# Eight low parts of the first mixer's weights made by VectorE, where GpSimd made them

## The chip, the cores and the metric

The kernel runs on one core of a Trainium2 chip. The metric is the device time of one execution in microseconds. Times of single instructions come from one profiled execution.

## The reference

Two transformer blocks over 256 tokens of width 1024 in float32. The change lies in the first mixer of the first block, which computes

```python
h = rmsnorm(x, norm1_w)
rq, rk, rv, rg, mq, mk, mv, ga, gb = split(h @ w_in)      # widths 512 512 1024 1024 512 512 512 1024 1024
ret = silu(rg) * retention(rotary(rq), rotary(rk), rv)    # 4 heads, chunks of 128
a = ret @ w_ret_out
b = moba_attention(rmsnorm(mq), rmsnorm(mk), mv) @ w_moba_out   # 8 heads of 64; with 256 tokens one block, causal softmax
x = x + (sigmoid(ga) * a + sigmoid(gb) * b) @ w_o
```

Behind it come a gated feed-forward of width 2816, and the second block: four more such feed-forwards, a forgetting attention, a latent attention (MLA) and two gated side inputs. All products are wanted at float32 precision.

## The kernel before

**Split products.** TensorE multiplies rounded float32 (fp32r). Each float32 weight is therefore split in two: a high part, its rounding, and a low part, the weight less the high part; activations are split likewise. A product is the sum of three matmuls (`mm3`, lines 582 to 584): high by high, high by low, low by high.

**Units.** All weights come through a list of 252 units (`weight_units`), in the order of their use, most of 128 x 2048 numbers: one MB, in two DMAs of 512 KB that SP issues. A unit u goes through three raw buffers (`w_raw[u % 3]`) and four buffers of high and low parts (`slots[u]`). ScalarE makes the high part (line 1326 in `split_to`, counted by `w_hi_done`) once the unit has landed and the unit before it in its slot has been used. VectorE (`lo`, line 1859) or GpSimd (line 507) makes the low part and counts up `w_lo_done[u % 3]`. TensorE waits for that count before it uses the low part, and SP waits for it before it loads unit u + 3 into the same raw buffer. `pool_units` is the set of units whose low part GpSimd makes; VectorE skips these in its own `split_to`, GpSimd's loop skips all others.

**Order on each engine.** Every engine runs one list of instructions in the order in which it is written. `split_to(n)` issues the parts of all units below n that aren't issued yet; `ahead(stage)` is `split_to` up to three units past the stage's last one. On VectorE these calls stand between the other work: `ahead("mv0")` ahead of the scaling of the MoBA queries and keys (line 2224 is its first instruction: mean and epsilon for the inverse roots), `split_to(unit_at["ga0"][0] + RING)` between the gating of the retention (line 2271) and the attention, and in the attention one unit per head, through this list:

```python
            fill = {s: [lambda u=u: split_to(u + RING)] for s, u in
                    zip((0, 1, 2, 3, 4, 7, 8), [*unit_at["ga0"], *unit_at["ga1"], *unit_at["gb0"], *unit_at["gb1"]][1:])}
```

The entries of key s run on VectorE after the softmax and the scaling of head s + 1.

**Units around the change** (each stage here has two units, moba_out0 and moba_out1 have one): rq0 0, 1; rk0 2, 3; rv0 4, 5; rv1 6, 7; mq0 8, 9; mk0 10, 11; mv0 12, 13; rg0 14, 15; rg1 16, 17; ga0 18, 19; ga1 20, 21; gb0 22, 23; gb1 24, 25; ret_out0 26, 27; ret_out1 28, 29; moba_out0 30; moba_out1 31; w_o 32 to 35; the feed-forward from 36.

**MoBA attention.** `attention("moba", ...)` runs a pipeline over heads. In step s TensorE makes the scores of head s (line 893, into bank 4 or 5), transposes the weights of head s - 1 (line 578, once VectorE has scaled them), for every second head multiplies a pair of heads by their values (line 915), and then fills in projections: step 0 the second unit of ga0, steps 1 and 2 ga1, 3 the first unit of gb0, 4 and 5 the second of gb0 (a tile of tokens each) with transposes of the retention's output in step 4, 6 only such transposes, 7 and 8 gb1. VectorE, per head: masked scores and their maximum (line 2085), the reciprocal of the sum (line 2092), the scaling of the weights (line 2096), for every second head the low part of an output (line 2104), and what `fill` holds. ScalarE, per head: what its own `fill` holds (the high part of a unit, the tanh of a gate), the exponentials (line 1334, like most of its work), a copy of the turned weights and of an output. The high part of unit 25 stands in its list ahead of the tanh of gb0 and the exponentials of head 6, behind the exponentials of head 5.

Of the kernel before, what the change touches and what calls it, by code (L numbers as in the profile page):

```python
# [48 lines left out]
RMS_EPS, LN_EPS, GN_EPS = 1e-6, 1e-5, 1e-5  # L49
ALPHA = float((2 * 2) ** 0.25)  # L50
NEG = -1e30
POOL_STAGES = ("ga1", "gb0", "gb1", "kv_up", "fox_q1", "fox_k1", "fox_q2", "fox_k2", "fox_v5", "fox_q3", "fox_k3", "uq",
               "mla_oa0", "mla_oa1")

F32 = mybir.dt.float32
# [124 lines left out]
def build(nc, dram, marks):  # L180
# [3 lines left out]
    units, unit_at = weight_units(dram)  # L184
# [14 lines left out]
    def up_cols(f):  # L199
        return slice(HB - gate_cols(f).start, 2 * HB - gate_cols(f).start)  # L200

    pool_units = {u for u, unit in enumerate(units) if unit[0] in POOL_STAGES}
    pool_units |= {unit_at[f"ffn{f}"][0] + 1 for f in (0, 1, 2, 4)}
    pool_units |= {unit_at[stage][i] for stage, i in (("rg0", 1), ("moba_out1", 0), ("fox_v4", 0),
                                                      ("fox_o0", 0), ("fox_o1", 0),
                                                      ("ple_g00", 0), ("ple_g10", 0))}
    ffn_w = [(dram["w_ffn_gate"], dram["w_ffn_up"], dram["w_ffn_down"])]
# [2325 lines left out]
```

## Time and profile before

| | us |
|---|---|
| median of 3 runs | 1500.1 (1499.11 to 1500.71) |
| the profiled execution | 1500.31 |
| its span, first to last instruction | 1498.2 |
| TensorE busy | 1477.7 |
| VectorE busy | 928.7 |
| ScalarE busy | 793.2 |
| GpSimd busy, 56 instructions | 190.1 |

The profile follows one execution. PE is TensorE, DVE VectorE, ACT ScalarE, POOL GpSimd, SP the engine whose queue issues the loads of weights. L2271 is line 2271 of the kernel. A matmul's end is modelled, so neighbouring ones overlap in the rows. Times are microseconds from the start of the span unless marked ns. The mean granted clock of TensorE is 0.998 of full speed.

### The profile page before, as it was taken

How to read it: one execution, taken by the hardware profiler on the slowest of the kernel's cores; microseconds unless marked ns; L12 is line 12 of the kernel's file. 1: busy time of each engine (PE TensorE's matmuls, PEld its weight loads, DVE VectorE, ACT ScalarE, POOL GpSimd, SP SyncE). 2: the span in 40 equal slices, each digit the busy share in tenths (PEclk: the TensorE clock that was granted, in tenths of full speed). 3: DMA queues.
4: the chain of work that ended last, by engine and by line, in shares of the span. 5: the costliest groups of instructions: out<-in, count | busy, mean ns of one | idle time of the engine just before them, and what ended most of it. 6: DMA issues, size and time to landing. Idle time of an engine off the chain costs nothing.

```text
span 1498.2 us, 21332 instructions
## 1 busy us (share of the span) xinstructions
PE 1477.7 (99%) x8040; PEld 1275.1 (85%) x8040; DVE 928.7 (62%) x1207; ACT 793.2 (53%) x975; POOL 190.1 (13%) x56
## 2 busy tenths in 40 slices
PE   8999999999999999999999999999999999999997
PEld 6888788888888888888888888888888998888886
DVE  7476455666656665525766668765666565766667
ACT  6436545444444445666544456644446664544456
POOL 0015211000040000372100001000005441100010
PEclk9999999999999999999999999999999999999999
DMA  9545456666546555552565557565555336555562
GB/s 345 185 142 177 135 177 198 217 195 196 186 159 214 184 186 177 187 170 85 196 222 183 186 194 228 176 223 184 186 192 164 124 113 197 196 197 188 184 216 71
DMA packets 187545, 274.73 MB, mean 183 GB/s; under 512 B 10048, under 2 KB 137184, under 8 KB 187488
## 3 DMA queue, kind: packets, MB, share of 16 engines
q1 hardware_dynamic: 183568, 262.77, 53.3%
q10 hardware_dynamic: 3920, 11.18, 2.3%
q8 instruction: 39, 0.64, 0.2%
q14 instruction: 18, 0.15, 0.0%
HBM read 272.83 MB, written 1.05 MB: 183 GB/s over the span
## 4 chain that ended last, share of the span: by engine, by line
PE 91%; DVE 5%; ACT 2%; issue 1%; DMA 0%; DVEq 0%; SPq 0%; ACTq 0%
PE bank L720 23%; PE bank L727 12%; PE acc L584 7%; PE acc L583 7%; PE acc L582 7%; PE bank L582 6%; PE bank L584 6%; PE bank L583 6%; PE bank L766 3%; PE acc L893 2%; PE acc L578 2%; PE bank L629 2%; PE bank L636 2%; PE bank L644 2%; DVE w_lo L1859 1%; PE bank L951 1%
## 5 line engine op out<-in xcount | busy, mean ns | idle before, releaser
L1859 DVE TENSOR_TENSOR w_lo<-w_raw,w_hi 128x2048 fp32r<-128x2048 f32 (+1 forms) x208 | 472.9, 2278 | 165.6 <-ACT w_hi L1410 121.3
L720 PE MATMUL bank<-xT,w_hi 128*128 128x512 f32 x1520 | 361.3, 390 | 0.0
L507 POOL TENSOR_TENSOR w_lo<-w_raw,w_hi 128x2048 fp32r<-128x2048 f32 (+1 forms) x41 | 176.9, 4321 | 1264.9 <-ACT w_hi L1326 1264.9
L720 PEld LDWEIGHTS bank<-xT,w_hi 128*128 128x128 f32 x1520 | 282.6, 188 | 56.6
L1410 ACT ACTIVATE w_hi<-w_raw 128x2048 fp32r<-128x2048 f32 x145 | 276.4, 1906 | 0.0
L1326 ACT ACTIVATE w_hi<-w_raw 128x2048 fp32r<-128x2048 f32 (+4 forms) x105 | 189.4, 1817 | 29.1 <-PE bank L584 10.1
L727 PEld LDWEIGHTS bank<-xT,w_lo 128*128 128x128 f32 x1520 | 189.3, 192 | 3.9
L727 PE MATMUL bank<-xT,w_lo 128*128 128x256 f32 x1520 | 191.4, 284 | 0.0
L582 PE MATMUL acc<-w_hi,sTh 128*128 128x512 f32 x400 | 155.9, 390 | 0.0
L583 PE MATMUL acc<-w_lo,sTh 128*128 128x512 f32 x400 | 155.9, 390 | 0.0
L584 PE MATMUL acc<-w_hi,sTl 128*128 128x512 f32 x400 | 155.8, 390 | 0.0
L582 PE MATMUL bank<-w_hi,xT 128*128 128x512 f32 (+1 forms) x304 | 119.8, 394 | 0.2 <-DVE w_lo L1859 0.2
L584 PE MATMUL bank<-w_hi,xT 128*128 128x512 f32 (+1 forms) x304 | 117.1, 385 | 0.0
L583 PE MATMUL bank<-w_lo,xT 128*128 128x512 f32 (+1 forms) x304 | 116.9, 384 | 0.0
L1421 ACT ACTIVATE squares<-bank 128x512 f32<-128x512 f32 x50 | 29.9, 597 | 139.6 <-PE bank L727 139.6
L1432 ACT ACTIVATE sTh<-hid 128x512 fp32r<-128x512 f32 x45 | 28.4, 632 | 135.0 <-PE acc L584 135.0
L584 PEld LDWEIGHTS acc<-w_hi,sTl 128*128 128x128 f32 x400 | 75.1, 188 | 15.6
L582 PEld LDWEIGHTS acc<-w_hi,sTh 128*128 128x128 f32 x400 | 75.1, 188 | 15.4
L583 PEld LDWEIGHTS acc<-w_lo,sTh 128*128 128x128 f32 x400 | 75.1, 188 | 15.4
L1421 ACT ACTIVATE tanh<-bank 128x512 f32<-128x512 f32 x45 | 26.8, 596 | 106.2 <-PE bank L720 106.2
L582 PE MATMUL bank<-xT,w_hi 128*128 128x256 f32 x271 | 78.7, 290 | 0.3 <-ACT arena L1334 0.3
L584 PE MATMUL bank<-xT,w_lo 128*128 128x256 f32 x271 | 76.8, 283 | 0.0
(231 smaller groups left out, 2030.0 us busy)
## 6 DMA issues: line engine op xcount, KB each, us to landing
w_raw<-in_ffn_w_in SPq DMA_DIRECT2D x176, 512.0 KB, 4.4
w_raw<-in_ffn_w_out SPq DMA_DIRECT2D x88, 512.0 KB, 4.2
w_raw<-in_w_in SPq DMA_DIRECT2D x52, 512.0 KB, 4.8
w_raw<-in_fox_w_in SPq DMA_DIRECT2D x24, 512.0 KB, 4.6
w_raw<-in_w_ffn_gate SPq DMA_DIRECT2D x22, 512.0 KB, 4.7
w_raw<-in_w_ffn_up SPq DMA_DIRECT2D x22, 512.0 KB, 4.5
w_raw<-in_w_ffn_down SPq DMA_DIRECT2D x22, 512.0 KB, 4.2
w_raw<-in_ple_w_gate SPq DMA_DIRECT2D x16, 512.0 KB, 4.5
```

The lines of the kernel that those rows point to most:

```text
L507: pool.tensor_tensor(w_lo[s][:, 0:cols], w_raw[u % RING][:, 0:cols], w_hi[s][:, 0:cols].bitcast(F32), ALU.subtract).then_inc(w_lo_done[u % ...
L578: mm = pe.matmul(bank[b][:, c:c + P], src, ident, is_transpose=True, start=True, stop=True)
L582: pe.matmul(out, ah, bh, start=first, stop=False, skip_group_check=biased)
L583: pe.matmul(out, ah, bl, start=False, stop=False, skip_group_check=biased)
L584: return pe.matmul(out, al, bh, start=False, stop=last, skip_group_check=biased)
L720: mm = pe.matmul(bank[b + m], wh[:, k, m], both, start=k == 0 and not narrow_first, stop=k == KD - 1 and narrow_first, skip_group_check=na ...
L727: mm = pe.matmul(bank[b + m][:, S:], wl[:, k, m], xTh[:, k], start=k == 0 and narrow_first, stop=k == KD - 1 and not narrow_first, skip_gr ...
L766: mm = pe.matmul(out, (xTl if part == 1 else xTh)[:, k, tok], both[:, k], start=part == 0 and k == 0, stop=last and k == KD - 1)
L1326: nc.scalar.activation(hi, raw, ACT.Copy).then_inc(w_hi_done, 1)
L1410: nc.scalar.activation(w_hi[slots[u]][:, :], w_raw[u % RING][:, :], ACT.Copy).then_inc(w_hi_done, 1)
L1421: nc.scalar.activation(dst.rearrange("p (m n) -> p m n", m=2), low[:, b:b + 2, S:], ACT.Copy)\
L1859: nc.vector.tensor_tensor(w_lo[s][:, 0:cols], w_raw[u % RING][:, 0:cols], w_hi[s][:, 0:cols].bitcast(F32), ALU.subtract).then_inc(w_lo_don ...
```

## The change

The set `pool_units` loses eight units of the first mixer: the second unit of rg0 (15), both of ga1 (20, 21), of gb0 (22, 23) and of gb1 (24, 25), and that of moba_out1 (31). Since VectorE's `split_to` takes every unit that isn't in the set, VectorE issues these eight low parts, each where its `split_to` reaches the unit's number. The instruction is the same on the other engine. GpSimd keeps the units behind the first mixer.

```diff
-POOL_STAGES = ("ga1", "gb0", "gb1", "kv_up", "fox_q1", "fox_k1", "fox_q2", "fox_k2", "fox_v5", "fox_q3", "fox_k3", "uq",
+POOL_STAGES = ("kv_up", "fox_q1", "fox_k1", "fox_q2", "fox_k2", "fox_v5", "fox_q3", "fox_k3", "uq",
                "mla_oa0", "mla_oa1")
...
-    pool_units |= {unit_at[stage][i] for stage, i in (("rg0", 1), ("moba_out1", 0), ("fox_v4", 0),
+    pool_units |= {unit_at[stage][i] for stage, i in (("fox_v4", 0),
                                                       ("fox_o0", 0), ("fox_o1", 0),
                                                       ("ple_g00", 0), ("ple_g10", 0))}
```

## Rows read from the trace of the kernel before

**Rows 1.** The page: busy time of each engine, and the chain that ended last.
```profile
PE 1477.7 (99%) x8040; PEld 1275.1 (85%) x8040; DVE 928.7 (62%) x1207; ACT 793.2 (53%) x975; POOL 190.1 (13%) x56
...
PE 91%; DVE 5%; ACT 2%; issue 1%; DMA 0%; DVEq 0%; SPq 0%; ACTq 0%
```

**Rows 2.** The page's costliest groups: busy us, mean ns; idle before, and its releaser.
```profile
L1859 DVE TENSOR_TENSOR w_lo<-w_raw,w_hi 128x2048 fp32r<-128x2048 f32 (+1 forms) x208 | 472.9, 2278 | 165.6 <-ACT w_hi L1410 121.3
...
L507 POOL TENSOR_TENSOR w_lo<-w_raw,w_hi 128x2048 fp32r<-128x2048 f32 (+1 forms) x41 | 176.9, 4321 | 1264.9 <-ACT w_hi L1326 1264.9
```

**Rows 3.** Waits of TensorE, 60 to 260 us: us in total, times, longest.
```profile
PE acc L578 <- DVE arena L2096: 1.1, 2, 0.8
```

**Rows 4.** Timeline of GpSimd: start, us taken, instruction, count, idle before.
```profile
86.62 4.90 POOL L507 TENSOR_TENSOR w_lo<-w_raw,w_hi 128x2048 fp32r<-128x2048 f32 x1 [83.58 <-ACT w_hi L1326]
122.97 5.03 POOL L507 TENSOR_TENSOR w_lo<-w_raw,w_hi 128x2048 fp32r<-128x2048 f32 x1 [31.45 <-ACT w_hi L1326]
132.67 9.18 POOL L507 TENSOR_TENSOR w_lo<-w_raw,w_hi 128x2048 fp32r<-128x2048 f32 x2 [4.67 <-ACT w_hi L1326]
...
161.28 4.55 POOL L507 TENSOR_TENSOR w_lo<-w_raw,w_hi 128x2048 fp32r<-128x2048 f32 x1 [7.46 <-ACT w_hi L1326]
192.79 5.12 POOL L507 TENSOR_TENSOR w_lo<-w_raw,w_hi 128x2048 fp32r<-128x2048 f32 x1 [26.96 <-ACT w_hi L1326]
```

**Rows 5.** Timeline of VectorE ahead of the attention.
```profile
84.77 2.29 DVE L1859 TENSOR_TENSOR w_lo<-w_raw,w_hi 128x2048 fp32r<-128x2048 f32 x1 [1.59 <-ACT w_hi L1326]
86.97 4.59 DVE L2224 TENSOR_SCALAR rsqrt_v<-rsqrt_b 128x32 f32<-128x32 f32 x1
...
119.93 1.41 DVE L2271 SCALAR_TENSOR_TENSOR arena<-tanh,neg_mean,arena 128x512 f32<-128x512 f32 x2
...
124.78 4.44 DVE L2271 SCALAR_TENSOR_TENSOR arena<-squares,neg_mean,arena 128x512 f32<-128x512 f32 x2
129.14 0.28 DVE L2085 CUSTOM_DVE_ANT_0 arena<-acc,mask 128x128 f32<-128x128 f32 x1
```

**Rows 6.** Timeline of ScalarE: high parts of units 14, 15 and of 25.
```profile
82.83 3.71 ACT L1326 ACTIVATE w_hi<-w_raw 128x2048 fp32r<-128x2048 f32 x2
...
159.30 1.91 ACT L1326 ACTIVATE w_hi<-w_raw 128x2048 fp32r<-128x2048 f32 x1
```

**Rows 7.** Timeline of VectorE in the attention: heads 2, 4, 5 and 6.
```profile
138.56 0.29 DVE L2085 CUSTOM_DVE_ANT_0 arena<-acc,mask 128x128 f32<-128x128 f32 x1 [2.97 <-PE acc L893]
...
154.38 0.74 DVE L2096 TENSOR_SCALAR arena<-acc,exp_rsum 128x128 f32<-128x128 f32 x2
157.09 0.29 DVE L2085 CUSTOM_DVE_ANT_0 arena<-acc,mask 128x128 f32<-128x128 f32 x1 [1.97 <-PE acc L893]
...
161.83 0.29 DVE L2085 CUSTOM_DVE_ANT_0 arena<-acc,mask 128x128 f32<-128x128 f32 x1 [1.77 <-PE acc L893]
...
163.73 0.74 DVE L2096 TENSOR_SCALAR arena<-acc,exp_rsum 128x128 f32<-128x128 f32 x2
```

**Rows 8.** Timeline of TensorE: scores and transposes of weights in three steps.
```profile
130.69 0.82 PE L893 MATMUL acc<-arena 128*128 128x128 f32 x4
131.82 0.55 PE L578 MATMUL acc<-ident,arena 128*128 128x128 f32 x3 [0.32 <-DVE arena L2096]
...
160.98 0.82 PE L893 MATMUL acc<-arena 128*128 128x128 f32 x4
161.63 0.49 PE L578 MATMUL acc<-ident,arena 128*128 128x128 f32 x3
...
162.90 0.82 PE L893 MATMUL acc<-arena 128*128 128x128 f32 x4
164.53 0.55 PE L578 MATMUL acc<-ident,arena 128*128 128x128 f32 x3 [0.80 <-DVE arena L2096]
```

**Rows 9.** Windows at the end: length, busy of each engine, granted clock, DMA.
```profile
1490.00:1492.00 2.00, 0.00 (x0) 0.00 (x0) 1.76 (x8) 1.88 (x4) 0.00 (x0) 1.00 0.00 0
1492.00:1494.00 2.00, 0.00 (x0) 0.00 (x0) 1.38 (x4) 1.46 (x3) 0.00 (x0) 0.86 0.00 0
```

## Prediction

> **What bounds the kernel now.** I read the page first: TensorE is busy for 1477.7 of 1498.2 us, and the chain that ended last is 91% TensorE, 5% VectorE and 2% ScalarE [rows 1]. So work taken from or given to another engine counts only where TensorE waits for it. The groups then give the price of a low part: 2278 ns on VectorE and 4321 ns on GpSimd (4.6 us for a unit of 2048 columns, the mean holds shorter ones) [rows 2]. The waits between 60 and 260 us, the stretch that holds all eight moved units, show what there is to win: TensorE stood for 1.1 us, two times, before transposes of softmax weights (line 578) that VectorE had to scale (line 2096), the longer time 0.8 us [rows 3]. The timeline of GpSimd says when the moved parts run now [rows 4], those of VectorE and ScalarE what stands beside them [rows 5 to 7], and that of TensorE where the two waits lie [rows 8]: the first pair of transposes of the MoBA attention at 131.82 and the seventh at 164.53. I count heads from 0, and units as the list of the kernel does: 15 is the second of rg0, 20 and 21 ga1, 22 and 23 gb0, 24 and 25 gb1, 31 moba_out1.
>
> **What is removed.** GpSimd loses eight instructions: units 15, 20, 21 and 22 (one row of 9.18), 23, 24, 25 and 31. Nothing else is in its queue there: its next instruction, for unit 37 at about 234, is for the feed-forward, and stays. No DMA, no matmul and no ScalarE instruction is added or removed. SP's loads wait for low parts (three raw buffers), so they shift; I come to that.
>
> **What is added.** Eight instructions of line 1859 on VectorE. Back to back one takes the queue for 2.20 us (84.77 to 86.97) [rows 5]. That is 17.6 us of VectorE in a stretch where it is busy for little more than half. Each stands at the place where its loop calls `split_to`, and holds up whatever comes behind it until ScalarE's high part is there.
>
> **Unit 15 and the lock.** It now stands in front of line 2224. Its high part is the second of the two of ScalarE that begin at 82.83 and end at 86.54 [rows 6], so it runs from 86.97 to 89.17. Today line 2224, a scalar operation on 32 columns, takes 4.59 us from 86.97, to 91.56 [rows 5], and the GpSimd unit that began at 86.62 ends at 91.52 [rows 4]: I read this as VectorE held until GpSimd is through. Without it the line should take some 0.2 us, so VectorE is at 89.4 where it now is at 91.56: 2.2 us early although it does more.
> The Trainium skill, "SBUF — State Buffer", section "SBUF: two separate sides", says that GpSimd and VectorE share one pair of ports as an exclusive lock for a whole instruction, against VectorE operations in a two-port mode or with two SBUF inputs. The trace agrees here, with 4.59 us for line 2224.
>
> **Unit 20 and the first softmax.** The same shows at line 2271: the pair at 119.93 takes 1.41 us, the same shape at 124.78 takes 4.44 [rows 5], beside the GpSimd unit that runs from 122.97 to 128.00 [rows 4]. That is 3.03 us given back, for one unit of 2.20. Even if none of the 2.2 us won at unit 15 were left (VectorE waits several times for ScalarE and TensorE in between), VectorE would be through line 2271 at 124.78 + 1.41 = 126.2 and through unit 20 at 128.4, before the 129.14 at which the first softmax begins now; if all of it is left, at 126.2. So the weights of head 0 come 0.8 to 3.0 us earlier. TensorE uses 0.48 of it: in a step without a wait the transposes begin 0.65 us after the scores (160.98 to 161.63), so at 130.69 + 0.65 = 131.34 where it is 131.82 today [rows 8]. Term: -0.48 us. More can't come of it: TensorE has no other wait before this.
>
> **Units 21, 22, 23.** In the attention VectorE makes unit 21 after the weights of head 1, 22 after those of 2, 23 after those of 3. It then stands idle till TensorE has the next scores: 2.97 us before 138.56, and more the two times after it [rows 7]; a unit of 2.20 fits each time. TensorE asks for each one or two steps later, with a margin of over 2 us. Cost 0, covered by this idle time; with the cover gone each would cost up to 2.20.
>
> **Unit 24.** The weights of head 4 end at 154.38 + 0.74 = 155.12, and the softmax of head 5 begins at 157.09, 1.97 later [rows 7]. The unit ends at about 157.26: 0.17 us late. TensorE isn't waiting there, but ScalarE's exponentials of head 5 and its high part of unit 25 behind them are late by as much.
>
> **Unit 25, the one that costs.** Its high part is made by ScalarE from 159.30 to 161.21 [rows 6], behind the exponentials of head 5, the turned weights and the output of a pair; GpSimd starts at 161.28 [rows 4]. The softmax of head 6 begins at 161.83 [rows 7], as soon as TensorE has the scores (from 160.98, four matmuls in 0.82). In the new order unit 25 stands ahead of that softmax and waits for its high part till 161.21 + 0.17 = 161.38; it runs from 161.42 to 163.62, and only then the softmax begins: 163.62 - 161.83 = 1.79 us late. TensorE has no large fill in this step, only transposes and the scores of head 7 (from 162.90), and already waits 0.80 for the weights of head 6 [rows 8]. So the whole 1.79 goes into the path: softmax, exponentials and scaling take 2.64 from 161.83 to 163.73 + 0.74 [rows 7], the transposes begin at 166.3. Term: +1.79 us; without the 0.17 of unit 24 1.62. Bounds: 0, if something lets ScalarE make the high part earlier (nothing in its order does), and 1.79 + 0.5 if the queue of ScalarE, which evacuates the gates between, is held up too.
>
> **Unit 31 and the loads.** GpSimd makes it from 192.79, when its high part is there [rows 4]; on VectorE it follows unit 30, and TensorE uses it only behind the rest of ret_out1 and the whole of moba_out0. Cost 0; without that cover 2.20. The raw buffers come free later for units 22, 23 and 24, in which units 25, 26 and 27 are loaded. Unit 22 is through at about 138.56 + 2.64 + 2.20 = 143.4 (a softmax and its scaling take 2.64, below), some 1.5 us later than now; a load lands about 5 us after its issue; and ScalarE converts unit 25 at 159.30 [rows 6], 11 us behind. Unit 24 is through at 157.3, so unit 27 lands by about 163, and ScalarE takes 26 and 27 only behind the transposes of 164.53 [rows 8]. Cost 0; if one of these loads were over its slack, ScalarE and then TensorE would wait for the excess.
>
> **Sum.** The profiled execution took 1500.31 us, its span is 1498.2, 2.1 lie around it, and it is 0.2 above the median of 1500.1. So 1500.31 - 0.48 + 1.79 = 1501.6, and on the scale of the median 1501.4: 1.3 us, or 0.09%, slower. Behind the attention TensorE, the other engines and the loads are all tied to each other, and I see nothing that would take a delay back.
>
> The Trainium skill, "GPSIMD Engine Reference", section "Engine selection", advises VectorE for elementwise work, GpSimd being about two times slower. The trace agrees, with 4.6 [rows 4] against 2.28 us [rows 2], but the place in VectorE's queue decides: by the page alone the change would be a gain, and I weigh that as the first rival.
>
> **Rivals.** A measurement of this kernel can tell about 0.2%, 3 us, from no change.
> *The gain alone.* The lock's end gives 0.48 us and unit 25 costs nothing, because the softmax of head 6 isn't late or the delay is taken back behind it: 1499.6. For it: VectorE gets over 7 us of held time back. Against: that time lies before 129.14, and the wait at 164.53 exists already [rows 8]. If all 1.1 us of waits for weights [rows 3] went too: 1499.0, so a gain of over 0.2% is out of reach by this road.
> *No lock (the other side).* The 4.59 and 4.44 us are long for another reason and stay. Then units 15 and 20 come on top, 4.4 us, the weights of head 0 are 4.4 us later, and TensorE waits for them: 1500.1 + 4.4 + 1.8 = 1506.3. It decides, as slower by over 0.2%, once the weights of head 0 come 1.2 us later than now. Against it: the ends of both long operations follow those of the GpSimd units, and line 2096, which reads PSUM, takes 0.74 both beside GpSimd (163.73) and without it (154.38) [rows 4, 7].
> *The clock falls.* The pause at 163.7 grows from 0.8 to 2.6 us. At the end of the kernel the granted clock falls from 2.4 to 1.2 GHz only after TensorE has stood since 1490: 1.00 till 1492, 0.86 in the next two [rows 9], so some 3.7 us of idleness were borne at the high level. Should it fall after 2.6, each us at 1.2 GHz costs half a us, and 3.4 us there make it slower by over 0.2%; 8 us would give 1505.4.
>
> **How the numbers follow.** Forecast 0.80, gain alone 0.09, no lock 0.06, clock 0.05. The forecast's own spread (1.62 to 2.3 for unit 25, 0 to 0.48 won, and some 0.8 of scatter of a median, as the three runs show) is 1500.3 to 1503.0. The range reaches down to the first rival: 1499.5 to 1503.0. Slower by over 0.2%, above 1503.1: the last two rivals and the forecast's upper edge, 0.12. Faster by over 0.2%, below 1497.1: no case, 0.03 for what I missed. Within 0.2%: 0.85.
>
> **What would show it.** GpSimd busy about 152 us (190.1 less the eight units: 4.90, 5.03, 9.18 for two, 4.55, 5.12 and two of 4.6 [rows 4]) with 48 instructions; line 1859 216 times; VectorE at 928.7 + 18.2 - 7.4 = 939.5 us (eight of 2.28, less 4.4 and 3.0). Line 2224 at about 0.2 us, the second pair of line 2271 at 1.4. No wait of TensorE at 131, one of about 2.6 us at 163 to 166, and unit 25 on VectorE right before the softmax of head 6. Wrong, if that softmax still begins with its scores; if line 2224 stays long; if new waits of TensorE stand between 132 and 158, or before the ret_out and moba_out matmuls.

## The result, and the profile after

The median of 22 runs is 1502.81 us (1500.36 to 1504.07) against 1500.09 (1499.11 to 1500.96), slower by 2.7 us or 0.18%. The means lie 2.1 us apart, a ratio of 1.0014 with a 95% interval of 1.0008 to 1.0020: clear of noise, and inside the 0.2% that I had called no change. The 22 runs aren't one heap: ten lie from 1500.36 to 1501.18, none between 1501.2 and 1502.7, and twelve from 1502.71 to 1504.07. The profiled execution, 1503.06 us with a span of 1501.2, is one of the upper group.

The page of the changed kernel, busy times and the two costliest groups (columns as in [rows 1, 2]):

```profile
PE 1479.3 (99%) x8040; PEld 1275.8 (85%) x8040; DVE 938.5 (63%) x1215; ACT 793.6 (53%) x975; POOL 152.1 (10%) x48
...
L1859 DVE TENSOR_TENSOR w_lo<-w_raw,w_hi 128x2048 fp32r<-128x2048 f32 (+1 forms) x216 | 490.9, 2278 | 168.9 <-ACT w_hi L1410 121.4
...
L507 POOL TENSOR_TENSOR w_lo<-w_raw,w_hi 128x2048 fp32r<-128x2048 f32 (+1 forms) x33 | 138.9, 4216 | 1305.9 <-ACT w_hi L1326 1305.9
```

GpSimd and VectorE are where the forecast put them (152 and 939.5 us). Waits of TensorE from 60 to 260 us in the changed kernel, answering to [rows 3]:

```profile
PE acc L578 <- DVE arena L2096: 2.4, 1, 2.4
PE acc L915 <- ACT squares L1334: 0.7, 1, 0.7
PE bank L582 <- DVE w_lo L1859: 0.2, 1, 0.2
```

One wait for scaled weights in place of two, and longer than both together. The timeline of VectorE ahead of the attention, answering to [rows 5]:

```profile
85.08 4.50 DVE L1859 TENSOR_TENSOR w_lo<-w_raw,w_hi 128x2048 fp32r<-128x2048 f32 x2 [1.59 <-ACT w_hi L1326]
89.50 0.17 DVE L2224 TENSOR_SCALAR rsqrt_v<-rsqrt_b 128x32 f32<-128x32 f32 x1
...
122.87 1.41 DVE L2271 SCALAR_TENSOR_TENSOR arena<-squares,neg_mean,arena 128x512 f32<-128x512 f32 x2
124.20 2.28 DVE L1859 TENSOR_TENSOR w_lo<-w_raw,w_hi 128x2048 fp32r<-128x2048 f32 x1
126.40 0.28 DVE L2085 CUSTOM_DVE_ANT_0 arena<-acc,mask 128x128 f32<-128x128 f32 x1
```

Units 14 and 15 run back to back, line 2224 takes 0.17 us where it took 4.59, the second pair of line 2271 takes 1.41 where it took 4.44, and with unit 20 in between the first softmax begins at 126.40 instead of 129.14. Then the attention, VectorE at heads 5 and 6 (answering to [rows 7]), with units 24 and 25:

```profile
154.80 2.28 DVE L1859 TENSOR_TENSOR w_lo<-w_raw,w_hi 128x2048 fp32r<-128x2048 f32 x1
156.99 0.28 DVE L2085 CUSTOM_DVE_ANT_0 arena<-acc,mask 128x128 f32<-128x128 f32 x1
...
161.13 2.29 DVE L1859 TENSOR_TENSOR w_lo<-w_raw,w_hi 128x2048 fp32r<-128x2048 f32 x1 [1.17 <-ACT w_hi L1326]
163.34 0.28 DVE L2085 CUSTOM_DVE_ANT_0 arena<-acc,mask 128x128 f32<-128x128 f32 x1
```

VectorE waits 1.17 us for ScalarE's high part of unit 25, spends 2.2 on the low part, and only then, at 163.34, begins the softmax whose scores TensorE began at 160.74. TensorE in the same steps (answering to [rows 8]):

```profile
131.01 0.82 PE L893 MATMUL acc<-arena 128*128 128x128 f32 x4
131.66 0.49 PE L578 MATMUL acc<-ident,arena 128*128 128x128 f32 x3
...
160.74 0.82 PE L893 MATMUL acc<-arena 128*128 128x128 f32 x4
161.39 0.49 PE L578 MATMUL acc<-ident,arena 128*128 128x128 f32 x3
...
162.79 0.82 PE L893 MATMUL acc<-arena 128*128 128x128 f32 x4
166.03 0.74 PE L578 MATMUL acc<-ident,arena 128*128 128x128 f32 x3 [2.41 <-DVE arena L2096]
...
179.87 0.38 PE L578 MATMUL acc<-ident,arena 128*128 128x128 f32 x2
```

And the row of the kernel before that answers to the last one, the transposes of head 7:

```profile
176.82 0.49 PE L578 MATMUL acc<-ident,arena 128*128 128x128 f32 x3
```

Subtracting row from row of [rows 8] gives the account. The scores of head 1 are 131.01 - 130.69 = 0.32 us late: the execution was that much behind before the attention. Those of head 6 are 160.74 - 160.98 = 0.24 early: 0.56 won at head 0. The transposes of head 6 are 166.03 - 164.53 = 1.50 late: 1.74 lost at unit 25. The transposes of head 7 are 179.87 - 176.82 = 3.05 late: another 1.55, in a stretch where TensorE waited for nothing. The windows say why (columns as in [rows 9]):

```profile
164.00:166.00 2.00, 0.00 (x0) 0.00 (x0) 0.94 (x4) 1.99 (x7) 0.00 (x0) 1.00 0.73 226
166.00:168.00 2.00, 1.98 (x11) 1.11 (x11) 1.71 (x6) 0.59 (x2) 0.00 (x0) 0.56 0.79 298
168.00:170.00 2.00, 2.00 (x9) 1.50 (x6) 1.20 (x5) 2.00 (x7) 0.00 (x0) 0.59 0.00 0
170.00:172.00 2.00, 2.00 (x11) 1.63 (x10) 2.00 (x4) 1.19 (x1) 0.00 (x0) 1.00 0.00 0
```

The granted clock fell to its lower level, 1.2 GHz, about when the pause ended, and came back to 2.4 before 170. A mean between 1.00 and 0.50 is a mixture of the two levels: 0.56 and 0.59 over two stretches of 2 us are 3.4 us at the lower one. At half speed these would cost 1.7 us of dense work; the rows show 1.55. The multiplication of a pair of heads takes 0.87 us in the kernel before and 1.55 here:

```profile
166.69 1.55 PE L915 MATMUL acc<-arena 128*64 128x256 f32 x8
```

0.32 - 0.56 + 1.74 + 1.55 = 3.05 us, against the 3.0 between the two spans. So the profile names two costs, a delay and a fall of the clock. If the fall comes in 12 of 22 runs, the average cost is 1.74 - 0.56 + 1.55 x 12/22 = 2.0 us, against the 2.1 between the means. The experiments were to tell whether both hang on unit 25, and whether the fall is what parts the two groups.

### The profile page after: what moved, and what is told of

Same layout as the page of the kernel before. It is cut to its first block, busy times and chain, and to the rows that moved or that the text cites. A ratio compares the mean times of both kernels' runs of the same rounds, so it can differ in the third digit from the quotient of the medians.

```text
span 1501.2 us, 21332 instructions
## 1 busy us (share of the span) xinstructions
PE 1479.3 (99%) x8040; PEld 1275.8 (85%) x8040; DVE 938.5 (63%) x1215; ACT 793.6 (53%) x975; POOL 152.1 (10%) x48
## 4 chain that ended last, share of the span: by engine, by line
PE 93%; DVE 4%; ACT 2%; issue 0%; DMA 0%; DVEq 0%; SPq 0%; ACTq 0%
PE bank L720 23%; PE bank L727 12%; PE bank L582 7%; PE bank L584 7%; PE bank L583 7%; PE acc L584 7%; PE acc L582 7%; PE acc L583 7%; PE bank L766 3%; PE acc L893 2%; PE acc L578 2%; PE bank L629 2%; PE bank L636 2%; PE bank L644 2%; PE bank L951 1%; DVE tanh L1943 1%
## 5 line engine op out<-in xcount | busy, mean ns | idle before, releaser
L1859 DVE TENSOR_TENSOR w_lo<-w_raw,w_hi 128x2048 fp32r<-128x2048 f32 (+1 forms) x216 | 490.9, 2278 | 168.9 <-ACT w_hi L1410 121.4
L507 POOL TENSOR_TENSOR w_lo<-w_raw,w_hi 128x2048 fp32r<-128x2048 f32 (+1 forms) x33 | 138.9, 4216 | 1305.9 <-ACT w_hi L1326 1305.9
```

Of the source, the lines that this page charges most:

```text
L507: pool.tensor_tensor(w_lo[s][:, 0:cols], w_raw[u % RING][:, 0:cols], w_hi[s][:, 0:cols].bitcast(F32), ALU.subtract).then_inc(w_lo_done[u % ...
L1859: nc.vector.tensor_tensor(w_lo[s][:, 0:cols], w_raw[u % RING][:, 0:cols], w_hi[s][:, 0:cols].bitcast(F32), ALU.subtract).then_inc(w_lo_don ...
```

## The experiments

Each kernel ran 11 times, `e7_longer` 8 times, beside 30 or 33 runs of the kernel before on the same chip. The first four shared one set of these (median 1499.92), the last four another (1500.08). Ratios are of means, as above. A single time of the kernel before lies up to a microsecond to either side of the median.

**Unit 25 back on GpSimd** (`e1_without_25`), the other seven as changed:

```diff
-    pool_units |= {unit_at[stage][i] for stage, i in (("fox_v4", 0),
+    pool_units |= {unit_at[stage][i] for stage, i in (("gb1", 1), ("fox_v4", 0),
```

> The change without unit 25 (second unit of gb1), whose low part GpSimd makes again; the other seven are made by VectorE. Queue theory: the delay of the softmax of head 6 is gone but for the 0.2 us of unit 24, TensorE waits about 0.9 us for the weights of head 6 and not at all for those of head 0, the clock stays at 2.4 GHz through the attention, and the time is 1500.1 - 0.5 + 0.1 = 1499.7 in every run, with no run above 1501.5. Rival, the cost lies in the other seven units or behind the first mixer: the time stays near 1502, and runs above 1502.5 go on appearing.

Measured: 1499.69 us (1498.68 to 1500.29), ratio 0.9998 (0.9989 to 1.0007). The highest run is below the lowest of the change. Waits of TensorE, 60 to 260 us:

```profile
PE acc L915 <- ACT squares L1334: 0.7, 1, 0.7
PE acc L578 <- DVE arena L2096: 0.7, 1, 0.7
```

The scores and the transposes of head 6:

```profile
160.26 0.82 PE L893 MATMUL acc<-arena 128*128 128x128 f32 x4
163.81 0.55 PE L578 MATMUL acc<-ident,arena 128*128 128x128 f32 x3 [0.67 <-DVE arena L2096]
```

The wait at head 6 is 0.7 again, 0.2 less than I had expected with unit 24 in place, and from the scores to the transposes it is 3.55 us, as in the kernel before. Seven moved units cost nothing together; the loss hangs on the eighth.

**Unit 25 alone on VectorE** (`e2_only_25`), the kernel before otherwise:

```diff
+    pool_units -= {unit_at["gb1"][1]}
     ffn_w = [(dram["w_ffn_gate"], dram["w_ffn_up"], dram["w_ffn_down"])]
```

> The kernel before with unit 25 alone moved to VectorE. Queue theory: TensorE waits about 0.8 + 1.6 = 2.4 us for the weights of head 6, the wait of 0.3 us for those of head 0 and the held lines 2224 and 2271 (4.6 and 4.4 us) stay; time 1500.1 + 1.6 = 1501.7 in the runs where the clock holds and about 1.5 us more where it falls in the pause, so that the runs stand in two groups. Rival, the other seven units cost: at most 0.3 us above before.

Measured: 1501.53 us (1500.87 to 1504.91), ratio 1.0015 (1.0006 to 1.0024). Two groups again, though by the times alone the gap between them is narrow: seven runs from 1500.87 to 1501.90, four at 1502.25, 1502.42, 1504.03 and 1504.91. What parts them is the mean clock, 0.999 in all of the seven and 0.996 to 0.998 in the four. The profiled execution is one in which the clock held, with the pause of 2.4 us all the same (lines are one further down in this kernel; the second and third lines are the scores and the transposes of head 6):

```profile
PE acc L579 <- DVE arena L2097: 2.7, 2, 2.4
```
```profile
160.35 0.82 PE L894 MATMUL acc<-arena 128*128 128x128 f32 x4
165.51 0.55 PE L579 MATMUL acc<-ident,arena 128*128 128x128 f32 x3 [2.41 <-DVE arena L2097]
```

One unit alone makes both the delay, 5.16 us from the scores to the transposes where it was 3.55, and the second group. The change shows fewer runs in its lower group (10 of 22) than this kernel (7 of 11), a difference that so few runs can't establish.

**Unit 25 one step later** (`e3_25_later`), behind the softmax and scaling of head 6:

```diff
-                    zip((0, 1, 2, 3, 4, 7, 8), [*unit_at["ga0"], *unit_at["ga1"], *unit_at["gb0"], *unit_at["gb1"]][1:])}
+                    zip((0, 1, 2, 3, 5, 7, 8), [*unit_at["ga0"], *unit_at["ga1"], *unit_at["gb0"], *unit_at["gb1"]][1:])}
-            fill[5] = [lambda: xT_evac("ret", (0,), slot0=8)]
+            fill[5].append(lambda: xT_evac("ret", (0,), slot0=8))
```

> The whole change, with unit 25 one step later in VectorE's list: behind the softmax and scaling of head 6, ahead of the transposed retention output. Queue theory: the softmax of head 6 begins with its scores again, the wait of TensorE for its weights is about 0.9 us as before, that of head 0 gone; unit 25 delays the softmax of head 7 by 2.2 us, which TensorE needs only some 10 us later; 1499.7, faster than before by 0.4 and faster than the change by 2 to 3. Rival, it is VectorE's load and not the place that costs: no better than the change, 1502 or more.

Measured: 1500.99 us (1500.16 to 1501.36), ratio 1.0005 (0.9996 to 1.0014). Half a miss: no run lies above 1502, but the time is 1.3 us over the 1499.7 expected. The timeline of TensorE shows it:

```profile
163.92 0.55 PE L578 MATMUL acc<-ident,arena 128*128 128x128 f32 x3 [0.67 <-DVE arena L2096]
...
166.72 0.50 PE L582 MATMUL bank<-w_hi,xT 128*128 128x512 f32 x1 [1.45 <-DVE xT L1899]
```

The transposes of head 6 are on time, but the first matmul of gb1 waits 1.45 us for line 1899, the low part of the turned retention output, which VectorE reads out of the bank that gb1 writes next. I had looked only at the softmax behind the unit, not at the evacuation between them. The delay had been handed from one reader to the next.

**TensorE kept at work in the pause** (`e4_busy_pe`): the change, with nine matmuls whose products are not used, into the idle output bank:

```diff
+            def keep_busy(n):
+                need("pe", "o", "moba", 3)
+                u = unit_at["gb1"][0]
+                pe.wait_ge(w_hi_done, u + 1)
+                wh = w_hi[slots[u]][:, :].rearrange("p (k n) -> p k n", k=4)
+                for i in range(n):
+                    pe.matmul(bank[7], xTh[:, i % 4, 0:P], wh[:, i % 4], start=True, stop=True)
...
-                       6: [lambda: to_xT("ret", ro, (1,), b0=2)], 7: [gb1[0]]}, {8: [gb1[1]]})
+                       6: [lambda: to_xT("ret", ro, (1,), b0=2), lambda: keep_busy(9)], 7: [gb1[0]]}, {8: [gb1[1]]})
```

> The whole change, with nine extra matmuls (fp32r, 512 columns, into a bank whose content is done with; their products are not used) between the turned retention output and the scores of head 7, so that TensorE works for some 2.0 us of the pause. The softmax of head 6 is as late as in the change. Clock theory: the clock doesn't fall, the runs above 1502.5 vanish, and the time is that of the change's lower group plus little, 1500.7 to 1501.5. Rival, the runs above 1502.5 have another cause than the pause: they go on appearing in about half of the runs, and the median is 1502.8 or above.

Measured: 1501.08 us (1500.18 to 1501.76), ratio 1.0007 (0.9998 to 1.0016); no run of 11 in the upper group, where the change had 12 of 22. Its TensorE:

```profile
162.24 2.33 PE L1032 MATMUL acc<-w_hi,xT 128*128 128x512 f32 x9
164.40 0.82 PE L893 MATMUL acc<-arena 128*128 128x128 f32 x4
165.55 0.55 PE L578 MATMUL acc<-ident,arena 128*128 128x128 f32 x3 [0.33 <-DVE arena L2104]
166.03 0.87 PE L915 MATMUL acc<-arena 128*64 128x256 f32 x8
```

The transposes of head 6 begin 1.74 us later than in `e1_without_25` (165.55 against 163.81 there, with the scores of head 6 within 0.01 us of each other), so the delay is all there; the pair of heads takes 0.87, so the clock is not down. Adding work to TensorE took 1.7 us off the change's median, and no run shows a mean clock below 0.998. What brings the upper group is TensorE's idleness in the pause, and not the delay.

**Units 15 and 20 alone** (`e5_only_15_20`), the kernel before otherwise:

```diff
+    pool_units -= {unit_at["rg0"][1], unit_at["ga1"][0]}
     ffn_w = [(dram["w_ffn_gate"], dram["w_ffn_up"], dram["w_ffn_down"])]
```

> The kernel before with units 15 and 20 alone moved to VectorE. Lock theory: line 2224 takes 0.2 us instead of 4.6, the second pair of line 2271 1.4 instead of 4.4, the weights of head 0 come some 3 us earlier, TensorE's wait for them (0.32 us) goes, that for head 6 stays at 0.8: 1499.4 to 1499.6, 0.3 to 0.5 below before. No-lock rival: both lines stay long, the weights of head 0 come 4.4 us later, and the time is 1504.

Measured: 1499.72 us (1498.86 to 1500.28), ratio 0.9997 (0.9988 to 1.0006); the difference of 0.36 is of the expected size, but the interval holds 1. The instructions are beyond doubt (two lines of VectorE, one further down here; shortest, median and longest duration in ns):

```profile
L2225 DVE TENSOR_SCALAR rsqrt_v<-rsqrt_b x1: 174/174/174, 89.7 to 89.7; 128x32 f32<-128x32 f32 x1
```
```profile
L2272 DVE SCALAR_TENSOR_TENSOR arena<-squares,neg_mean,arena x2: 745/748/751, 123.1 to 123.7; 128x512 f32<-128x512 f32 x2
```

Both hold-ups go when nothing but the two GpSimd instructions beside them moves, though VectorE then has two more instructions.

**Half of unit 25 in the place** (`e6_half_25`); `lo_half(u, n)` is `lo` on one half of the columns, and unit 25 leaves the list of `fill`:

```diff
...
+            def first_half(u):
+                dve.wait_ge(w_hi_done, u + 1)
+                lo_half(u, 0)
+                split[0] = u + 1
...
+            fill[4] = [lambda: first_half(u25)]
+            fill[5] = [lambda: xT_evac("ret", (0,), slot0=8), lambda: lo_half(u25, 1)]
```

> The whole change, with unit 25 in two instructions of 1024 columns: the first where the change has it, ahead of the softmax of head 6, the second behind the first low part of the turned retention output. Queue theory: that softmax is 0.7 us late instead of 1.8, TensorE waits about 1.4 us for the weights of head 6, and the time is 1499.7 + 0.6 = 1500.3. Clock theory: with a pause of 1.4 us, between the 0.8 at which no run fell and the 2.4 at which about half did, few or no runs lie above 1502. Rival, any low part in that place costs the whole 1.7 us: 1501.3.

Measured: 1499.96 us (1498.96 to 1500.63), ratio 0.9999 (0.9990 to 1.0008), no run above 1500.7. TensorE waits 1.3 us at head 6:

```profile
PE acc L578 <- DVE arena L2110: 1.3, 1, 1.3
```

Half the block makes a wait of 1.34 us where it is 0.67 without it, 0.7 more, and no run as long as one with a fall. The delay is as expected; the median is 0.3 below the 1500.3 I had put down, which is within the scatter.

**A longer block in the place** (`e7_longer`): the first half of unit 25 is made twice, so VectorE has more ahead of the softmax of head 6, 1.1 us by plan and 1.3 in the trace:

```diff
...
+            def longer(u):
+                dve.wait_ge(w_hi_done, u + 1)
+                lo_half(u, 0)
+                settle()
+                lo(u)
+                split[0] = u + 1
...
+            fill[4] = [lambda: longer(u25)]
```

> The whole change, with the first half of unit 25 made once more ahead of it (1024 columns, 1.1 us longer in front of the softmax of head 6). Queue theory: TensorE waits about 3.6 us for the weights of head 6. Clock theory: the clock falls in nearly all runs, and the time is 1502.0 where it holds and 1503.5 to 1506 where it falls, in more than the 12 of 22 runs of the change. Rival, the two groups of the change come from something other than the length of the pause: the share of runs in the upper group stays near a half, 1.1 us higher than in the change.

Measured: 1504.80 us (1502.85 to 1505.38), ratio 1.0029 (1.0018 to 1.0040). All eight runs lie above the 1502.0 that I expected where the clock holds, but three of them, at 1502.85, 1503.32 and 1503.44, below the 1503.5 from which I expected falls. The mean clock is 0.996 or 0.997 in seven; the lowest run has 0.998 and lies within the scatter of 1502.0, so for it a fall isn't shown. In the profiled one TensorE pauses 3.7 us, and the lower level lasts 6.8 us, twice as long as in the change:

```profile
166.00:168.00 2.00, 0.72 (x3) 0.50 (x3) 1.69 (x5) 1.59 (x5) 0.00 (x0) 0.55 0.95 346
168.00:170.00 2.00, 2.00 (x10) 1.19 (x10) 0.96 (x5) 1.00 (x5) 0.00 (x0) 0.50 0.40 155
170.00:172.00 2.00, 2.00 (x6) 1.52 (x6) 1.95 (x6) 2.00 (x3) 0.00 (x0) 0.50 0.00 0
172.00:174.00 2.00, 2.00 (x8) 1.63 (x7) 2.00 (x2) 0.43 (x1) 0.00 (x0) 0.74 0.00 0
```

**Unit 25 behind the evacuation** (`e8_25_behind_turned`), the order of `e3_25_later` with the two entries of that step exchanged:

```diff
-                    zip((0, 1, 2, 3, 4, 7, 8), [*unit_at["ga0"], *unit_at["ga1"], *unit_at["gb0"], *unit_at["gb1"]][1:])}
-            fill[5] = [lambda: xT_evac("ret", (0,), slot0=8)]
+                    zip((0, 1, 2, 3, 7, 8), [unit_at["ga0"][1], *unit_at["ga1"], unit_at["gb0"][0], *unit_at["gb1"]])}
+            fill[5] = [lambda: xT_evac("ret", (0,), slot0=8), lambda: split_to(unit_at["gb1"][1] + 1)]
```

> The whole change, with unit 25 behind the first low part of the turned retention output, in the step of head 6. The run with it one place ahead had a new wait of TensorE of 1.5 us: the first matmul of gb1 for the bank from which that low part is read. Queue theory, mended: that wait goes, the softmax of head 6 is on time, TensorE waits 0.7 for its weights and 0 for those of head 0, no run's clock falls: 1499.5 to 1499.8, 0.2 to 0.5 below before and 3 below the change. Rival: wherever unit 25 stands in VectorE's list it costs a microsecond or more, 1501.

Measured: 1499.29 us (1498.27 to 1499.89), ratio 0.9995 (0.9986 to 1.0004): the lowest median of all, 0.8 us below before, though the interval doesn't exclude no difference, and 3.5 us below the change, whose lowest run lies above its highest. All eight units are on VectorE, which is as busy as in the change:

```profile
PE 1476.7 (99%) x8040; PEld 1274.1 (85%) x8040; DVE 938.6 (63%) x1215; ACT 793.5 (53%) x975; POOL 152.1 (10%) x48
```
```profile
162.51 0.74 DVE L2096 TENSOR_SCALAR arena<-acc,exp_rsum 128x128 f32<-128x128 f32 x2
163.17 1.28 DVE L1899 TENSOR_TENSOR xT<-bank,xT 128x512 fp32r<-128x512 f32 x2
164.37 2.28 DVE L1859 TENSOR_TENSOR w_lo<-w_raw,w_hi 128x2048 fp32r<-128x2048 f32 x1
166.56 0.28 DVE L2085 CUSTOM_DVE_ANT_0 arena<-acc,mask 128x128 f32<-128x128 f32 x1
```

The same 2.28 us, some 4 us later in the queue (3.8 behind the begin of the softmax of head 6, which is at 160.61 here), cost nothing.

## Why the prediction was right, and what it missed

**The removed and added work.** Counts and busy times came out as worked out: 48 and 216 instructions, VectorE 938.5 for 939.5 us.

**Unit 15, unit 20 and the lock.** Right. The term of -0.48 us measured 0.56 in the row-by-row account. The no-lock rival, that the long lines are long for another reason, is dead by `e5_only_15_20`. The first softmax came 2.7 us earlier, near the upper of my bounds, and as argued TensorE could use only the half microsecond.

**Units 21 to 24, 31 and the loads.** Right: with all of these moved and unit 25 left, `e1_without_25` is at 1499.69. For unit 24 I had 0.17 us of delay for the softmax of head 5; it begins 1.00 us behind its scores (155.99 to 156.99) where it was 0.86 (156.23 to 157.09), 0.14 late, and the wait at head 6 did not grow without unit 25.

**Unit 25.** The term of +1.79 measured 1.74, in the place and for the reason given. Without unit 24 the prediction had 1.62, and `e2_only_25` shows 5.16 - 3.55 = 1.61. The whole cost without the clock shows in the median of `e4_busy_pe`: 1501.08 against 1499.92, that is +1.16, where the sum said +1.3.

**The clock: what was missed.** The median missed the forecast of 1501.4 by 1.4 us because of the step "some 3.7 us of idleness were borne at the high level", which left a pause of 2.6 us looking safe and the rival with 0.05. The runs say otherwise: the pause of 2.4 us brought the clock down in about twelve of 22 runs of the change, as far as the two groups tell. The step fails twice. The reading of the row was off: 0.86 over 2 us is 1.4 us at the high level, not 1.7, so the clock fell at 1493.4, some 3.5 us after the last matmul. Above all, one pause in one execution bounds nothing. In the profiled execution of `e7_longer` the last matmul of the kernel ends at 1495.25 and the clock falls at 1497.4 (0.85 is 1.4 us of 2 at the high level), some 2.1 us later:

```profile
1494.97 0.28 PE L584 MATMUL bank<-w_hi,xT 128*128 128x256 f32 x1
```
```profile
1494.00:1496.00 2.00, 1.25 (x11) 1.04 (x9) 1.79 (x7) 0.70 (x2) 0.00 (x0) 1.00 0.13 48
1496.00:1498.00 2.00, 0.00 (x0) 0.00 (x0) 1.90 (x6) 1.90 (x3) 0.00 (x0) 0.85 0.00 0
```

In `e4_busy_pe` it is 2.0 us by the same reckoning, in `e2_only_25` and `e5_only_15_20` 4.5. The ends of ten executions so give 2.0 to 4.5 us for the same idleness, and a pause of 2.6 lies inside that. The mechanism was in the prediction, with a price of half a microsecond per microsecond at 1.2 GHz, which the trace bears out (3.4 us, 1.55 lost); its chance was off by a factor of ten.

The Trainium skill, "TensorE: Matmul & The Clock Gate", section "What's actually happening", says that the clock is set by how busy TensorE has been of late, and that the moments at which the chip judges this are not tied to the kernel, so that the same kernel differs from run to run. The runs agree in that much, with ten and twelve runs of one kernel in two groups; what decides for a single run, none of them shows.

**What was luck.** The median lies inside the range, 0.2 us below its upper end of 1503.0, and that end was put there for the spread of unit 25 and the scatter (added up as written, 1500.1 + 2.3 + 0.8, it would be 1503.2), not for the clock. With the runs in two groups, at about 1500.7 and 1503.3, the median falls into one or the other by a run or two. The direction and the delay were worked out; that the total stayed in the range wasn't.

**What stays open.** That each run of the upper group had a fall of the clock is inferred from the profiled executions (down in the change and in `e7_longer`, up in the attention of the seven others and of the kernel before) and from the groups; no trace of every run was taken. The mean clock on record for each run agrees, but is too coarse to prove it: it is 0.999 in eight of the ten lower runs of the change, and 0.998 or 0.996 in the twelve upper ones, but 0.998 in the other two as well, and in most runs of the kernel before, whose traced fall comes only behind the last matmul. The sizes of the groups aren't explained either. The lower group (median 1500.67) is 0.6 us over before, where the two terms ask for 1.2 and `e4_busy_pe` has it; and the groups lie 2.7 us apart, where the traced fall cost 1.55. In the five longest runs, 1503.90 to 1504.07, the mean clock is 0.996, as in the traced execution of `e7_longer` with its 6.8 us at the lower level, so they may have had a longer fall; that isn't shown. Only the average over all runs fits the account.

Runs above 1502 stand for runs with a fall except for the longer block, where runs at the high level would lie around 1502.0 as well.

| kernel | longest wait of TensorE at head 6, us | median, us | runs above 1502 |
|---|---|---|---|
| before | 0.8 | 1500.09 | 0 of 22 |
| the change | 2.4 | 1502.81 | 12 of 22 |
| unit 25 on GpSimd | 0.7 | 1499.69 | 0 of 11 |
| unit 25 alone | 2.4 | 1501.53 | 4 of 11 |
| one step later | 0.7 (1.5 at gb1) | 1500.99 | 0 of 11 |
| TensorE kept busy | 0.3 | 1501.08 | 0 of 11 |
| units 15 and 20 alone | 0.8 | 1499.72 | 0 of 11 |
| half of unit 25 | 1.3 | 1499.96 | 0 of 11 |
| longer block | 3.7 | 1504.80 | 8 of 8 |
| behind the evacuation | 0.7 | 1499.29 | 0 of 11 |

## What to carry to other kernels

The price of a piece of work moved to another engine is set by what stands behind it in that engine's queue: seven of eight equal units cost nothing together, the eighth cost 1.7 us, 1.5 one place later, and nothing some four microseconds later in the queue; look at every reader behind it, not only at the first. A pause of TensorE of some two microseconds in a dense stretch should be priced twice, once as a delay and once as a chance of a fall of the clock, and the median of several runs told from their groups. Take GpSimd's work off only where an instruction of VectorE beside it is held up, and see whether anyone was waiting for it.

## What the runs showed of the hardware that was not expected

A pause of 2.4 us was enough to bring the granted clock from 2.4 to 1.2 GHz in about half of the runs of one program, one of 3.7 in at least seven of eight, and pauses of 0.7 to 1.5 us in none of 55 runs of five kernels, as far as the times and mean clocks tell. At the end of the kernels the clock fell between 2.0 and 4.5 us after the last matmul. The fall cost 1.55 us in the traced execution. Useless matmuls in the pause made the changed kernel 1.7 us faster.
